# Four transformer layers on one core: gates applied per feed-forward block, modulation products moved, last token tile alone, transposes in halves, part-wise signals of the low halves

## The reference

```python
def first_block(...):                     # layer 0: GLA mixer, layer 1: chunk attention
    for i in range(DEPTH):
        sh1, sc1, g1, sh2, sc2, g2 = split(silu(c) @ w_ada[i] + b_ada[i], 6)
        u = x * (1.0 + sc1) + sh1
        y = gla_mixer(u, ...) if i % 2 == 0 else chunk_attention(u, ...)
        x = layer_norm(ALPHA * x + (1.0 + g1) * y, ln_g[i, 0], ln_b[i, 0])
        u = x * (1.0 + sc2) + sh2
        y = square(relu(u @ w1)) @ w2     # 1024 -> 4096 -> 1024
        x = layer_norm(ALPHA * x + (1.0 + g2) * y, ln_g[i, 1], ln_b[i, 1])

def second_block(...):                    # layer 0: even mixer (HGRN2 + pooling), layer 1: odd mixer (forgetting attention)
    for l in range(DEPTH):
        shift, scale, gate = split(silu(c_2) @ ada_w[l] + ada_b[l], 3)
        h = rms_norm(x, norm_g[l]) * (1.0 + scale) + shift
        x = x + gate * (even_mixer(h, ...) if l % 2 == 0 else odd_mixer(h, ...))
```

## Time and profile before

| | |
|---|---|
| median of 3 runs | 2098.42 us (2095.8 to 2101.23) |
| the profiled execution, its own time | 2097.66 us |
| its span in the trace | 2095.9 us |
| mean granted clock of TensorE | 0.927 |
| PE busy | 1883.9 us (90%), 9171 matmuls |
| DVE, ACT, POOL busy | 1059.4, 751.0, 764.8 us |
| DMA | 235.66 MB, mean 112 GB/s |

### The profile page before, as it was taken

How to read it: one execution, slowest core, us unless ns; L and a number is a source line. 1 busy time by engine, 2 the same in 40 slices (tenths; PEclk the granted TensorE clock), 3 DMA queues, 4 the chain that set the end, 5 groups by cost and what they waited for, 6 DMA issues and landing times. The chain is left out here.

```text
span 2095.9 us, 24931 instructions
## 1 busy us (share of the span) xinstructions
PE 1883.9 (90%) x9171; PEld 1518.5 (72%) x9171; DVE 1059.4 (51%) x1670; ACT 751.0 (36%) x1174; POOL 764.8 (36%) x577
## 2 busy tenths in 40 slices
PE   4998788899999969989879999996899889989888
PEld 3886467688888757767668888884777777767767
DVE  5543645655455651554475455548377722125552
ACT  3233234232222153545332223214434535544451
POOL 3443012655555233221435555542422342432221
PEclk7998789999999889998999999987999998999899
DMA  7772014444554112211255554431111221322111
GB/s 306 236 240 86 0 41 147 164 161 149 183 173 165 60 64 97 71 61 63 91 174 166 168 163 160 157 133 41 60 61 46 81 64 58 101 81 71 61 51 41
DMA packets 116325, 235.66 MB, mean 112 GB/s; under 512 B 8049, under 2 KB 25329, under 8 KB 115217
## 3 DMA queue, kind: packets, MB, share of 16 engines
q1 hardware_dynamic: 113200, 227.17, 32.6%
q10 hardware_dynamic: 3040, 7.34, 1.0%
HBM read 232.36 MB, written 2.13 MB: 112 GB/s over the span
## 5 line engine op out<-in xcount | busy, mean ns | idle before, releaser
L1956 POOL TENSOR_TENSOR wsp<-raw,wsp 128x512 fp32r<-128x512 f32 x528 | 753.8, 1459 | 1310.0 <-ACT wsp L178 1310.0
L194 PE MATMUL bank<-xT,wsp 128*128 128x512 f32 x2592 | 621.5, 400 | 36.7 <-POOL wsp L1956 25.7
L194 PEld LDWEIGHTS bank<-xT,wsp 128*128 128x128 f32 x2592 | 496.0, 193 | 154.8 <-POOL wsp L1956 29.4
L178 ACT ACTIVATE wsp<-raw 128x2048 fp32r<-128x2048 f32 x132 | 252.6, 1915 | 806.6 <-PE bank L194 336.1
L372 PE MATMUL bank<-wsp,hT 128*128 128x512 f32 x1536 | 360.9, 395 | 3.5 <-DVE h L486 3.5
L372 PEld LDWEIGHTS bank<-wsp,hT 128*128 128x128 f32 x1536 | 289.2, 188 | 72.5 <-issue 5.2
L194 PE MATMUL bank<-wsp,xT 128*128 128x512 f32 x1248 | 296.5, 396 | 11.1 <-POOL wsp L1956 11.1
L194 PEld LDWEIGHTS bank<-wsp,xT 128*128 128x128 f32 x1248 | 235.3, 190 | 62.6 <-POOL wsp L1956 11.9
L467 DVE TENSOR_TENSOR tok<-tok,bank 128x512 f32<-128x512 f32 x96 | 65.9, 687 | 147.7 <-PE bank L372 146.2
L447 DVE TENSOR_TENSOR h<-h 128x512 f32<-128x512 f32 x64 | 65.4, 1029 | 98.1 <-ACT h L405 97.8
L452 DVE TENSOR_TENSOR hT<-h,hT 128x512 fp32r<-128x512 f32 x64 | 97.5, 1581 | 25.7 <-ACT hT L410 25.7
(11 more groups left out here) (303 smaller groups left out, 2095.5 us busy)
## 6 DMA issues: line engine op xcount, KB each, us to landing
raw<-in_ff_w SPq DMA_DIRECT2D x64, 1024.0 KB, 5.4
ada_ring<-in_w_ada SPq DMA_DIRECT2D x48, 384.0 KB, 3.8
ada_ring<-in_ada_w SPq DMA_DIRECT2D x48, 384.0 KB, 3.8
ring<-in_w_ada SPq DMA_DIRECT2D x64, 256.0 KB, 6.2
raw<-in_odd_w_in SPq DMA_DIRECT2D x16, 1024.0 KB, 5.6
raw<-in_gla_w_in SPq DMA_DIRECT2D x12, 1024.0 KB, 7.6
raw<-in_att_w_in SPq DMA_DIRECT2D x12, 1024.0 KB, 5.1
...
```

The source lines that it names most:

```text
L178: act.activation(wsp[:, slot, 0], raw[:, slot], ACT.Copy).then_inc(hi_made, 1)
L194: mm = pe.matmul(out_ap, l, r, start=(start and n == 0), stop=(stop and n == 2))
L1956: ins = pool.tensor_tensor(wsp[:, slot, 1, k], raw[:, slot, k], wsp[:, slot, 0, k].bitcast(F32), ALU.subtract)
```

## The change

- The low part of a half is signalled by k: `lo_part` behind each of the first three, `lo_made` behind the fourth, and TensorE waits per k (`low_ready`).
- The first half of a stage's first panel runs in the order WAVE, which takes each k of `xT` when it is there (`first_half`).
- The last panel of gla_out, even_in, even_out and of the two attention outputs runs in the order LAST_FIRST: tile 3 alone at the end.
- The transposes between stages run in two halves of k, tile by tile (`pe_transposes_by_tile`); ScalarE's high parts of the next panel stand ahead of the last tile's normalisation (`act_normalised_tiles`).
- SyncE issues the feed-forward's second panel directly behind its first.
- The gate is applied to each block's result in `add` (two operations), the residual in the first block; `gated_sum` is gone. The last down product runs tile by tile over four banks (`down_last`).
- Of 48 modulation columns 32 are made: 16 ahead of the last down product; the other 16 behind it (feed-forward 1) or in attention's tail (feed-forward 0). The gate rows stand behind the last down product.
- `affine1` starts ahead of the root; ScalarE's normalising pass is dropped there.
- Pairs: in units without a weight piece the scores stand ahead of the transposes. HGRN: two first halves in a row. Fox: mean squares one piece earlier, roots earlier on ScalarE, the first split of q and k inside the loop.
- The result of the even and odd mixers is added by halves of columns, and the output is written in halves.

```diff
+        WAVE = [(k, t) for w in range(HK) for k in range(HK) for t in range(ST) if max(k, t) == w]
+        LAST_FIRST = ((0, 0), (1, 0), (2, 0), (0, 1), (1, 1), (2, 1), (3, 0), (3, 1))
...
+        def low_ready(pe, j, k):
+            if k < HK - 1:
+                pe.wait_ge(lo_part, (HK - 1) * j + k + 1)
+            else:
+                pe.wait_ge(lo_made, j + 1)
+        def first_half(pe, j, kind, free, free_at, ts):
+            for k, t in WAVE:
+                if t == 0:
+                    low_ready(pe, j, k)
+                    pe.wait_ge(ts["xT_ready"], ts["k0"] + k + 1)
+                if k == 0:
+                    pe.wait_ge(free, free_at + t + 1)
+                mm = pe_tile(pe, bank[t][:, :], 0, k, k, t, kind, k == 0, False)
+            mm.then_inc(w_used, 1)
...
+            if first:
+                first_half(pe, j, kind, free, free_at, ts)
+            for t, h in LAST_FIRST if last else [(t, h) for h in range(1 if first else 0, 2) for t in range(ST)]:
                 if h == 0:
...
+        def pe_transposes_by_tile(pe, ts, need, between=None):
+            s = TS[ts]
+            for part in range(2):
+                if part and between:
+                    between()
+                for t in range(ST):
+                    pe.wait_ge(s["tok_ready"], need + t)
+                    for k in range(HK * part, HK * part + HK):
+                        mm = pe.transpose(bank[k][:, t * P:t * P + P], tok[:, t, k * P:k * P + P], ident[:, :])
+                        if t == ST - 1:
+                            mm.then_inc(s["tr_done"], 1)
...
             for h in range(2):
                 sp_half(sp, b + h, h, W1[l][:, HK * h:HK * h + HK, 0:COLS])
+            for h in range(2):
+                up_half(0, h)
             for r, row in enumerate(rows):
                 sp.dma_start(brow[l][:, r], row.partition_broadcast(P)).then_inc(brow_ld, 16)
             ada_tiles(0, range(KT), True)
-            with sp.Fori(0, FB - 1) as i:
+            ada_tiles(1, range(4))
...
+            def down_last():
+                i, j = FB - 1, b + 4 * FB - 2
+                pe.wait_ge(s["hT_ready"], 4 * i + 4)
+                for t in range(ST):
+                    for n in range(2):
+                        m = 2 * t + n
+                        pe.wait_ge(s["acc_done"], 16 * i - 8 + 2 * m + 1 if m < ST else 16 * i + m - ST + 1)
+                        mm = down_tile(j, n, t, ST + m % ST)
+                        mm.then_inc(s["ff2_tile"] if t < 3 else w_used, 1)
...
-            pe_modcols(pe, acc, range(48), 0, mod_done)
+            pe_modcols(pe, acc, range(16), 0, mod_done)
+            down_last()
             r1, r2 = mod_rows[l]
-            pe_modrow(pe, acc, r1, 1, mod_done)
-            pe.matmul(bank[3][:, :], ones[:, :], acc[:, r2:r2 + COLS], start=True, stop=True).then_inc(mod_done, 1)
-            pe.wait_ge(mod_made, 4 + 4 * l + 1)
-            pe.matmul(bank[0][:, :], ones[:, :], acc[:, r2 + COLS:r2 + D], start=True, stop=True).then_inc(mod_done, 1)
-            down(FB - 1, last=True)
+            if l:
+                pe.wait_ge(mod_made, 8)
+                pe_modcols(pe, acc, range(24, 40), 0, mod_done)
+            pe.wait_ge(s["acc_done"], 16 * (FB - 1) + 6)
+            pe_modrow(pe, acc, r1, 4, mod_done)
+            pe.wait_ge(s["acc_done"], 16 * (FB - 1) + 8)
+            pe_modrow(pe, acc, r2, 6, mod_done)
...
+                c = slice(n * COLS, n * COLS + COLS)
                 for t in range(ST):
-                    y = tok[:, t, n * COLS:n * COLS + COLS]
+                    y, m = tok[:, t, c], 16 * i + 8 * n + 2 * t
                     if t < 3:
                         dve.wait_ge(s["ff2_tile"], 6 * i + 3 * n + t + 1)
                     else:
                         dve.wait_ge(w_used, base[f"ff{l}"] + 4 * i + 4 + n + 1)
+                    dve.tensor_tensor(htmp[l][:, t % 2], bank[4 + t][:, :], gate[:, c], ALU.mult).then_inc(s["acc_done"], 1)
+                    dve.wait_ge(s["acc_done"], m + 1)
                     if peel:
-                        ins = dve.tensor_copy(y, bank[4 + t][:, :])
+                        ins = dve.scalar_tensor_tensor(y, x[:, t, c], ALPHA, htmp[l][:, t % 2], ALU.mult, ALU.add)
                     else:
-                        dve.wait_ge(s["acc_done"], 8 * i - 8 + 4 * n + t + 1)
-                        ins = dve.tensor_tensor(y, y, bank[4 + t][:, :], ALU.add)
+                        ins = dve.tensor_tensor(y, y, htmp[l][:, t % 2], ALU.add)
...
-            def gated_sum():
-
-                dve.wait_ge(s["acc_done"], 8 * (FB - 1))
-                for t in range(ST):
-                    dchain(dve, dve.tensor_tensor(tok[:, t], tok[:, t], gate[:, :], ALU.mult))
-                    dchain(dve, dve.scalar_tensor_tensor(tok[:, t], x[:, t], ALPHA, tok[:, t], ALU.mult, ALU.add))
...
+        def act_normalised_tiles(act, name, ready, q):
+            for t in range(ST):
+                if t == ST - 1:
+                    for slot in range(2):
+                        act_high(act, q, slot)
+                act_normalised(act, name, t, ready)
...
+                if u not in work and u + 1 < NU:
+                    scores(u + 1)
...
-                if u + 1 < NU:
+                if u in work and u + 1 < NU:
                     scores(u + 1)
+                if u == NU and in_tail:
+                    in_tail()
...
-                    if seq and i % 2:
-                        mean_square(ST * (seq - 1) + i // 2)
+                    if seq and i in MS_AFTER:
+                        mean_square(ST * (seq - 1) + MS_AFTER.index(i))
...
-        PIECE = ((0, 0), (0, 1), (1, 0), (1, 1), (2, 0), (3, 0), (2, 1), (3, 1))
+        PIECE = ((0, 0), (1, 0), (0, 1), (1, 1), (2, 0), (3, 0), (2, 1), (3, 1))
...
                     ins = pool.tensor_tensor(wsp[:, slot, 1, k], raw[:, slot, k], wsp[:, slot, 0, k].bitcast(F32), ALU.subtract)
-                ins.then_inc(lo_made, 1)
+                    ins.then_inc(lo_part if k < HK - 1 else lo_made, 1)
...
             def affine1(t):
 
+                dchain(dve, dve.scalar_tensor_tensor(tok[:, t], tok[:, t], mv[:, t, 0:1], lnrow[1][:, 0], ALU.subtract, ALU.mult))
                 dve.wait_ge(normed, t + 1)
-                dchain(dve, dve.tensor_tensor(tok[:, t], tok[:, t], lnrow[1][:, 0], ALU.mult))
-                dve.tensor_tensor(x[:, t], tok[:, t], lnrow[1][:, 1], ALU.add).then_inc(RS["even_in"]["x"], 1)
+                dve.scalar_tensor_tensor(x[:, t], tok[:, t], rstd[:, t:t + 1], lnrow[1][:, 1], ALU.mult, ALU.add)\
+                   .then_inc(RS["even_in"]["x"], 1)
```

310 lines of the change are left out of this document (158 added, 152 removed).

## The result

The changed kernel takes 2014.37 us in the median of four runs (2010.51 to 2015.38), the kernel before 2097.11 beside it; the ratio is 0.9604 (0.9577 to 0.9631). The profiled execution took 2010.51 us of its own time against 2097.66, a gain of 87.15 us; 2011 was forecast for the median, from a sum of -87.3 on the profiled execution. The profiled execution of the changed kernel is the fastest of its four; the medians are 82.7 us apart. So the total came out; several of its terms did not, and their errors cancelled, which is luck.

What follows compares the result with a forecast made beforehand. TensorE sets the end, with gains possible only in the seams, which cost idle time and a lower clock; terms sum to -87.3 against the profiled 2097.66, giving 2010.4, median 2011, range 1982 to 2052, forecast's chance 0.73.

Steps and rivals of the forecast that it cites:

- The seams: Two seams in front of the feed-forwards: halved transposes and products taking each k as it comes gain 4.8 us each, -9.6.
- The start of the feed-forward: Each feed-forward's start: second weight panel issued earlier, so its low half depends on the slot alone; 10 us each, -20.
- The end of the first feed-forward: Behind the first feed-forward loop: fewer columns, earlier down product, gate rows covering the last tile's normalisation; -23.5 us.
- The end of the second: Behind the second feed-forward loop: VectorE becomes the bound at 7.25 us a tile; -17 us.
- The moved columns: 16 modulation columns moved into attention's tail, where TensorE has no wait, so they are paid: +5.5 us.
- Scores ahead of transposes: Units without a weight piece: VectorE gets scores earlier, gaining 0.6 to 1 us in each of seventeen waits; -11 us.
- HGRN: HGRN stretch: three of four GpSimd waits mostly go through paired first halves and part-by-part signals; -8 us.
- The longest stays: HGRN stretch: the longest GpSimd wait, 5.66 us, remains because the last panel's new order gives its slot back 8.3 later.
- The odd mixer: Odd mixer: new waits on the mean square, four of 1.9 us, against a shorter wait for fkr; +2 us.
- Rival one: In the seams VectorE beside GpSimd becomes the bound, its operations slower; +40 us, 2051; chance 0.15.
- Rival two: Clock comes back: shorter idle lets the two long seams run at the upper level; -35 us, 1976; chance 0.07.
- Rival three: Feed-forward loop: VectorE's added operations exceed TensorE's 44.1 us a block; about 2110 at 51.7; chance 0.03.

Runs made afterwards that it cites:

- The three runs: Changed kernel with squares, weight loads and modulation tiles reordered at each feed-forward start, the last two also with moved columns and later mean squares: 2021.69, 2003.99, 2001.28 us.
- the reversed run: Changed kernel with the score products behind the transposes in every unit, as before the change: 2026.43 us, ratio 0.9672.
- the old-order run: Changed kernel with the last panels of gla_out, even_in, even_out and both attention outputs half by half again: 2023.23 us, ratio 0.9656.

## Why the prediction was right, point by point

**The seams** were right in size and only partly in reason: 4.4 gained for 4.8. The forecast credited the halved transposes, products that take each k as it comes, and a little clock; the run with the old panel order shows that 3.1 to 3.6 of it hang on tile 3 standing alone, without which the high parts collide with its normalisation.

**The start of the feed-forward** is the term that failed: 11.1 for 20. The step was "the low half depends on the slot alone"; true of the second panel, but the sum stopped there and did not ask what is late next. The first down product's weights were, by 4.3 to 4.8 us, through ScalarE's queue; the 8.86 us had covered that, and with the old order back that wait is gone. The three runs show that no single queue was to blame. The order alone is worth only 1.5 to 4 us.

**The end of the first feed-forward** was right in each step: start of the down product 9.1 behind the loop (9.13), 24.5 for the product (25.0), first attention product 8.2 to 10 later (8.3), 42 in all (42.4). What the forecast took as given is the 6.37 us of the last hidden block's low part: beside GpSimd's last low half its four operations take 6.35 again, where the same four at 379.14 take 2.49. Most of the two waits of 5.50 hangs on that; no run moves them apart. **The end of the second** was right as well: VectorE became the bound. Its tiles follow each other by 7.2 us, for 7.25 forecast, and TensorE waits 7.33 for its queue:

```profile
1374.01 0.68 DVE L534 TENSOR_TENSOR htmp<-bank,gate 128x512 f32<-128x512 f32 x1
...
1381.19 0.68 DVE L534 TENSOR_TENSOR htmp<-bank,gate 128x512 f32<-128x512 f32 x1
...
1394.56 6.39 PE L291 MATMUL bank<-ident,tok 128*128 128x128 f32 x32 [7.33 <-DVEq L2205]
```

**The moved columns** cost 3.9 as matmuls, for 5.5; the run that moved them shows 6.3 in the stage. **Scores ahead of transposes:** 11 was forecast, 12.2 is what the units gained beside the columns, and 15.0 what the reversed run lost. The term was built from 0.65 us of each wait; the reversed run shows that in attention the larger part is the same matmuls at a lower clock, which the forecast had left out there. So the size was right and the account was not.

**HGRN** was mis-sized, -12.1 for -8. "The longest stays" is wrong: all four waits for GpSimd went, also the 5.66 us. At that panel's start stands a wait of 2.23 with ScalarE as releaser, and one of 4.83 for GpSimd without the part-wise signals. The late slot is real (3 to 4 us in the old-order run), but a first part is enough to start. New waits of 2.54 and 1.57 for VectorE eat up part of it: 6.8 of the 12.1 are idle time, and 5.3 are TensorE's busy time (191.09 to 185.81 us) at a mean clock of 0.97 for 0.93, which the term had left out. **The odd mixer:** five waits of 1.94 to 2.02 where four of 1.9 were forecast, 2.59 at the end for 2.7. One of them is just over the 2 us that the forecast named as a sign of being wrong; it is a loss, and one that need not be.

**Rival one** did not come as a whole: during the last down product GpSimd is idle (26.66 us in the first feed-forward, 31.22 in the second), as the argument against it said. It came for the last tile at the second feed-forward's end, whose three operations cost 2.8 us more beside GpSimd. The first of the two affine operations for tile 0 and for tile 3:

```profile
1364.33 1.27 DVE L2254 SCALAR_TENSOR_TENSOR tok<-tok,mv,lnrow 128x1024 f32<-128x1024 f32 x1
...
1386.69 2.35 DVE L2254 SCALAR_TENSOR_TENSOR tok<-tok,mv,lnrow 128x1024 f32<-128x1024 f32 x1
```

And it came where the forecast did not put it, at the starts (four operations of the residual in the first feed-forward and three in the second, 1 us each). Its price over the whole kernel shows in two groups of the page, GpSimd's low part and the gated addition:

```profile
L2036 POOL TENSOR_TENSOR wsp<-raw,wsp 128x512 fp32r<-128x512 f32 x528 | 786.3, 1521 | 1189.6 <-ACT wsp L179 1189.6
...
L522 DVE TENSOR_TENSOR tok<-tok,htmp 128x512 f32<-128x512 f32 x96 | 91.6, 954 | 3.3
```

The added operation takes 0.954 us in the mean, between the 0.69 and 1.65 of the earlier trace rows, and GpSimd's low part went from 1.48 in the loop before to 1.61 (169.09 / 105). With the gate at the end again it is 1.48 (155.18 / 105), so GpSimd loses too. The Trainium skill ("SBUF — State Buffer", "SBUF: two separate sides") says of VectorE with two SBUF inputs and GpSimd that whichever starts first holds the shared pair of ports for its whole instruction while the other waits; the trace agrees in both directions, with 0.954 for 0.69 and 1.61 for 1.48. **Rival two** is partly in the result: about 27 us of the gain are left for the clock. The terms were made against whole seams and held part of it already; how much is not shown. **Rival three** was priced about rightly (57 measured for 45 by its rule), and 32.0 us a block is below where it decides.

The errors that cancelled: 9 too much at the starts; 4 too little in HGRN, 2.7 in the units and the columns, 2 in the stretch ahead of gla_out, where this change does little and which took 285 to 292 us over the runs. That they add up to nothing is luck. One sum of the forecast is off: its bounds added to one side give 1962 and 2060, not 1965 and 2071; the result lies inside either way.
